# Two SSM layers of a two-block network: the powers of B and the zeroing of the lag table moved from VectorE to GpSimd, with new task tables

## What is computed

```python
h = rmsnorm(x, norm_mix[i])
proj = h @ w_in[i]
q, k, v, cb, cc, cx, u, g = jnp.split(proj, IN_SPLITS, axis=-1)
q, k = partial_rope(q, ...), partial_rope(k, ...)
y_attn = sliding_window_attention(q, k, v, attn_sinks[i]) @ w_attn_o[i]
y_conv = (cb * short_conv(cc * cx, conv_w[i])) @ w_conv_o[i]
ys = jax.nn.gelu(s5_ssm(u, ssm_a_re[i], ssm_a_im[i], ssm_b_re[i], ...))
y_ssm = (ys * jax.nn.sigmoid(ys @ w_ssm_glu[i])) @ w_ssm_o[i]
x = x + (gates[0] * y_attn + gates[1] * y_conv + gates[2] * y_ssm) @ w_mix_o[i]
h = rmsnorm(x, norm_ffn[i])
x = x + (jax.nn.silu(gt) * up) @ w_ffn_out[i]        # gt, up = split(h @ w_ffn_in[i])
```

## Time and profile before

| what | value |
|---|---|
| median of 3 runs | 2157.72 us (2156.05 to 2157.94) |
| the profiled execution | 2156.08 us |
| its span, first to last instruction | 2154.3 us |
| granted TensorE clock | 0.999 |
| PE busy | 2131.7 us, 99% |
| DVE busy | 1640.0 us, 76% |
| ACT busy | 1212.4 us, 56% |
| POOL busy | 56.4 us, 3% |

### The profile page before, as it was taken

The page is one execution under the profiler, slowest core; times in us unless marked ns, Lnnn a source line. Parts: engine busy times, 40 slices in busy tenths (PEclk is TensorE's granted clock), DMA queues, the critical chain, the costliest instruction groups (busy, mean ns, idle before and its releaser), DMA issues.

```text
span 2154.3 us, 47945 instructions
## 1 busy us (share of the span) xinstructions
PE 2131.7 (99%) x18740; PEld 2074.0 (96%) x18740; DVE 1640.0 (76%) x2626; ACT 1212.4 (56%) x1823; POOL 56.4 (3%) x54
## 2 busy tenths in 40 slices
PE   9999999999999999999999999999999999999998
PEld 8999999999999999899999999999899999999998
DVE  8997877987778766778947877766678947877764
ACT  6656544556656445446658845445446658845443
POOL 0000000000000000000002200000000002200000
PEclk9999999999999999999999999999999999999999
DMA  7444655644456556554544466556554544465553
GB/s 250 157 136 150 201 190 185 198 156 148 138 167 216 186 194 208 169 167 147 176 158 148 148 202 208 185 188 211 174 166 148 173 160 147 148 199 189 185 189 127
DMA packets 102976, 376.54 MB, mean 175 GB/s; under 512 B 11680, under 2 KB 11808, under 8 KB 102304
## 3 DMA queue, kind: packets, MB, share of 16 engines
q1 hardware_dynamic: 101664, 368.66, 52.7%
q10 hardware_dynamic: 1152, 5.58, 0.7%
HBM read 373.14 MB, written 1.05 MB: 174 GB/s over the span
## 4 chain that ended last, share of the span: by engine, by line
PE 90%; DVE 6%; ACT 2%; issue 1%; DMA 0%; DVEq 0%; ACTq 0%
PE acc L772 25%; PE acc L774 24%; PE acc L773 24%; DVE w_lo L1806 2%; PE acc L891 1%; PE acc L893 1%; PE acc L892 1%; PE acc L836 1%; PE acc L838 1%; PE acc L837 1%; ACT w_hi L1325 1%; PE mid L1128 1%; PE mid L1227 1%; DVE pr L2565 0%; PE mid L959 0%
## 5 line engine op out<-in xcount | busy, mean ns | idle before, releaser
L1806 DVE TENSOR_TENSOR w_lo<-w_raw,w_hi 128x1024 fp32r<-128x1024 f32 x694 | 847.8, 1226 | 321.5 <-ACT w_hi L1325 313.3
L1325 ACT CAST w_hi<-w_raw 128x1024 fp32r<-128x1024 f32 x694 | 723.8, 1046 | 541.2 <-PE acc L774 476.6
L772 PE MATMUL acc<-h_hi,w_hi 128*128 128x256 f32 x2096 | 600.1, 286 | 0.1
L773 PE MATMUL acc<-h_lo,w_hi 128*128 128x256 f32 x2096 | 589.3, 281 | 0.0
L774 PE MATMUL acc<-h_hi,w_lo 128*128 128x256 f32 x2096 | 586.2, 280 | 0.0
L772 PE MATMUL acc<-g_hi,w_hi 128*128 128x256 f32 x1456 | 412.6, 283 | 0.8 <-DVE w_lo L1806 0.7
L773 PE MATMUL acc<-g_lo,w_hi 128*128 128x256 f32 x1456 | 407.9, 280 | 0.0
L774 PE MATMUL acc<-g_hi,w_lo 128*128 128x256 f32 x1456 | 407.6, 280 | 0.0
L772 PEld LDWEIGHTS acc<-h_hi,w_hi 128*128 128x128 f32 x2096 | 394.0, 188 | 6.3 <-issue 5.0
L774 PEld LDWEIGHTS acc<-h_hi,w_lo 128*128 128x128 f32 x2096 | 396.1, 189 | 0.0
L773 PEld LDWEIGHTS acc<-h_lo,w_hi 128*128 128x128 f32 x2096 | 395.5, 189 | 0.5
(11 more groups left out here) (443 smaller groups left out, 3454.6 us busy)
## 6 DMA issues: line engine op xcount, KB each, us to landing
w_raw<-weights_d SPq DMA_DIRECT2D x695, 512.0 KB, 3.6
p<-p_d ACTq DMA_DIRECT2D x3, 1080.0 KB, 8.5
rdec<-decay_d ACTq DMA_DIRECT2D x2, 768.0 KB, 7.6
p<-p_d SPq DMA_DIRECT2D x1, 1024.0 KB, 10.8
out_d<-work SPq DMA_DIRECT2D x4, 256.0 KB, 2.3
x_all<-x_d SPq DMA_DIRECT2D x1, 516.0 KB, 4.4
w_raw<-weights_d SPq DMA_DIRECT2D x2, 256.0 KB, 5.8
x_all<-x_d SPq DMA_DIRECT2D x1, 512.0 KB, 6.2
```

The source lines that it names most:

```text
L772: mm(dst, wh, hi[:, k, :], start=first and j == 0, stop=False)
L773: mm(dst, wh, lo[:, k, :], start=False, stop=False)
L1325: nc.scalar.copy(w_hi[:, slot, :], w_raw[:, slot, :]).then_inc(hi_done, 1)
L1806: tt(w_lo[:, slot, :], w_raw[:, slot, :], w_hi[:, slot, :].bitcast(F32), SUB).then_inc(lo_v, 1)
```

## The change

The powers 1 to 3 of B are made by GpSimd, by the same four operations each, in a list of its own ahead of its work for the second block. It waits for a new semaphore `v_fac`, which DVE's reciprocal at L2056 (the line after the last factor) raises, for B and C to have landed, and for the last raw slab. TensorE's `tr` 0 waits for the new `p_power`. The lag table is now a tile of 16x3x32 columns on the parameters of B and C, which are read by then: GpSimd zeroes it as soon as the powers, power 0 on ACT and the table from C on DVE are done, and `lag_copy` waits for `p_lag` and for the matmuls. DVE has neither `power` nor `lag_zero` any more. Both tables of tasks are new, with the same tasks otherwise.

```diff
-        lag = in_arena("lag", 91136, [P, PAIRS, STEP, PC])
+        lag = place("lag", [P, PAIRS, STEP - 1, PC], at=p_at + 4 * P1["b_re"][0])
...
+            mine = Products()
+            times = nc.gpsimd.tensor_tensor
+            def power(at, p):
+                i = STEP - 1 - p
...
+                times(by_re, b, l_re, ALU.mult)
+                times(by_im, b, l_im, ALU.mult).then_inc(p_step, 1)
+                pool.wait_ge(p_step, mine.next())
+                times(bs[0][:, :, i, :], by_re[:, 0, :, :], by_im[:, 1, :, :], ALU.subtract)
+                times(bs[1][:, :, i, :], by_re[:, 1, :, :], by_im[:, 0, :, :], ALU.add).then_inc(p_power, 1)
+                pool.wait_ge(p_power, at.n * 3 + p)
+            def powers(at):
+                if at.n == 0:
+                    pool.wait_ge(params, 16)
+                pool.wait_ge(v_fac, at.n + 1)
+                wait_used(pool, at, raw_end(at.n) - 1)
+                for p in range(1, STEP):
+                    power(at, p)
+            def lag_zero(at):
+                pool.wait_ge(a_power, at.n * 2 + 2)
+                pool.wait_ge(v_prep, at.n * 3 + 3)
+                nc.gpsimd.memset(lag[:, :, :, :], 0.0).then_inc(p_lag, 1)
+            for n in range(DEPTH):
+                at = Layer(False, n)
+                powers(at)
+                lag_zero(at)
...
-                    pe.wait_ge(v_power, at.n * 3 + 3)
+                    pe.wait_ge(p_power, at.n * 3 + 3)
...
-                act.wait_ge(v_lag, at.n + 1)
+                if j == 0:
+                    act.wait_ge(p_lag, at.n + 1)
+                    act.wait_ge(pe_lag, at.n + 1)
...
-                nc.vector.reciprocal(tiny[:, 17, :], tiny[:, 16, :])
+                nc.vector.reciprocal(tiny[:, 17, :], tiny[:, 16, :]).then_inc(v_fac, 1)
```

Of the tables, the entries up to the recurrence, layer 0:

```diff
-        3: (("mean",), ("roots",), ("h", 0), ("h", 1), ("h", 2), ("h", 3), ("lows",)),
-        5: (("rope", 0),),
-        6: (("rope", 1),),
-        7: (("prep_d",), ("rope", 2)),
-        9: (("scaled",),),
-        10: (("rope_mul", 0),),
+        3: (("mean",),),
+        4: (("roots",),),
+        6: (("h", 0), ("h", 1), ("h", 2), ("h", 3), ("lows",)),
+        9: (("prep_d",),),
         12: (("out_table",),),
-        14: (("power", 0),),
-        15: (("rope", 3), ("rope_mul", 1)),
-        17: (("rope", 4),),
-        18: (("double", 0), ("double", 1)),
-        19: (("rope_mul", 2),),
-        21: (("vt",), ("vt_copy",), ("power", 1)),
-        22: (("rope_mul", 3), ("rope_mul", 4)),
-        23: (("spread", 0),),
-        24: (("power", 2),),
-        26: (("power", 3), ("spread", 1), ("spread", 2), ("spread", 3)),
-        27: (("double", 2),),
-        28: (("tr", 0), ("tr", 1), ("tr", 2), ("tr", 3), ("tr", 4), ("double", 3), ("double", 4), ("tr", 5),
-            ("tr", 6), ("tr", 7), ("tr_copy", 0), ("tr_copy", 1), ("tr_copy", 2), ("tr_copy", 3), ("tr_copy", 4),
-            ("tr_copy", 5), ("tr_copy", 6), ("lag",), ("bu", 0), ("tr_copy", 7), ("lag_zero",), ("lag_copy", 0),
-            ("lag_copy", 1), ("double", 5), ("lag_copy", 2)),
-        29: (("bu", 1), ("rot", 0), ("bu", 2), ("bu", 3), ("rot", 1)),
-        30: (("rot", 2), ("rot", 3)),
...
+        3: (("mean",),),
+        4: (("roots",),),
+        6: (("h", 0), ("h", 1), ("h", 2), ("h", 3), ("lows",)),
+        9: (("prep_d",),),
         12: (("out_table",),),
-        14: (("power", 0),),
-        15: (("rope", 3), ("rope_mul", 1)),
-        17: (("rope", 4),),
-        18: (("double", 0), ("double", 1)),
-        19: (("rope_mul", 2),),
-        21: (("vt",), ("vt_copy",), ("power", 1)),
-        22: (("rope_mul", 3), ("rope_mul", 4)),
-        23: (("spread", 0),),
-        24: (("power", 2),),
-        26: (("power", 3), ("spread", 1), ("spread", 2), ("spread", 3)),
-        27: (("double", 2),),
-        28: (("tr", 0), ("tr", 1), ("tr", 2), ("tr", 3), ("tr", 4), ("double", 3), ("double", 4), ("tr", 5),
-            ("tr", 6), ("tr", 7), ("tr_copy", 0), ("tr_copy", 1), ("tr_copy", 2), ("tr_copy", 3), ("tr_copy", 4),
-            ("tr_copy", 5), ("tr_copy", 6), ("lag",), ("bu", 0), ("tr_copy", 7), ("lag_zero",), ("lag_copy", 0),
-            ("lag_copy", 1), ("double", 5), ("lag_copy", 2)),
-        29: (("bu", 1), ("rot", 0), ("bu", 2), ("bu", 3), ("rot", 1)),
-        30: (("rot", 2), ("rot", 3)),
-        31: (("scores", 0), ("mask", 0), ("scan",)),
-        33: (("scores", 1), ("scores", 2)),
-        34: (("mask", 1),),
-        35: (("mask", 2), ("scores", 3), ("mask", 3), ("scores", 4)),
-        36: (("mask", 4), ("turn",), ("scores", 5)),
-        38: (("scores", 6), ("scores", 7), ("mask", 5)),
-        39: (("mask", 6), ("mask", 7)),
-        40: (("out_power", 1), ("maxima",)),
+        13: (("power", 0),),
+        14: (("scaled",), ("rope", 0), ("rope", 1)),
+        15: (("rope", 2),),
+        16: (("rope_mul", 0),),
+        18: (("rope_mul", 1),),
+        19: (("rope", 3),),
+        21: (("rope", 4), ("rope_mul", 2), ("vt",), ("vt_copy",)),
+        22: (("rope_mul", 3), ("double", 0)),
+        23: (("rope_mul", 4), ("double", 1)),
+        24: (("tr", 0), ("double", 2), ("double", 3), ("tr_copy", 0)),
+        25: (("double", 4),),
+        26: (("tr", 1), ("tr", 2), ("tr_copy", 1), ("tr_copy", 2), ("spread", 0), ("tr", 3), ("tr_copy", 3)),
+        27: (("double", 5), ("tr", 4), ("tr", 5), ("tr_copy", 4), ("tr", 6), ("tr_copy", 5), ("tr_copy", 6),
+            ("spread", 1), ("spread", 2), ("spread", 3), ("tr", 7), ("tr_copy", 7)),
+        28: (("lag_copy", 0), ("lag_copy", 1), ("lag",), ("lag_copy", 2)),
+        29: (("bu", 0), ("bu", 1), ("bu", 2), ("bu", 3)),
+        30: (("rot", 0), ("rot", 1), ("rot", 2), ("rot", 3)),
...
```

Layer 1:

```diff
-        1: (("mean",), ("roots",)),
-        3: (("scaled",), ("h", 0), ("h", 1), ("h", 2), ("h", 3), ("lows",)),
-        4: (("rope", 0), ("rope_mul", 0), ("rope", 1)),
-        5: (("power", 0), ("rope_mul", 1)),
-        7: (("rope", 2), ("rope", 3)),
-        8: (("rope_mul", 2), ("power", 1)),
-        9: (("rope_mul", 3), ("spread", 0), ("rope", 4)),
-        10: (("rope_mul", 4), ("vt",), ("vt_copy",)),
-        11: (("spread", 1), ("power", 2)),
-        13: (("power", 3),),
-        16: (("tr", 0), ("tr", 1), ("tr", 2), ("tr_copy", 0)),
-        17: (("tr_copy", 1),),
-        18: (("tr_copy", 2), ("tr", 3), ("tr_copy", 3), ("tr", 4), ("tr_copy", 4), ("tr", 5), ("tr_copy", 5)),
-        20: (("tr", 6), ("tr", 7), ("lag",), ("spread", 2), ("spread", 3), ("tr_copy", 6), ("tr_copy", 7),
-            ("lag_zero",)),
-        21: (("bu", 0), ("bu", 1), ("rot", 0), ("lag_copy", 0), ("lag_copy", 1), ("lag_copy", 2)),
...
+        1: (("mean",), ("roots",), ("power", 0)),
+        2: (("rope", 0),),
+        3: (("h", 0), ("h", 1), ("h", 2), ("h", 3), ("lows",)),
+        4: (("scaled",), ("rope", 1), ("rope", 2)),
+        5: (("rope_mul", 0),),
+        6: (("rope_mul", 1),),
+        8: (("rope", 3),),
+        9: (("spread", 0),),
+        10: (("rope_mul", 2), ("rope", 4), ("vt",), ("spread", 1), ("vt_copy",)),
+        12: (("rope_mul", 3), ("rope_mul", 4)),
+        14: (("tr", 0),),
+        16: (("tr", 1), ("tr", 2), ("spread", 2), ("tr_copy", 0)),
+        17: (("tr_copy", 1), ("tr_copy", 2), ("tr", 3)),
+        19: (("tr_copy", 3), ("tr", 4), ("tr_copy", 4), ("tr", 5), ("tr_copy", 5), ("tr", 6), ("tr_copy", 6)),
+        20: (("spread", 3), ("tr", 7)),
+        21: (("tr_copy", 7), ("lag",), ("bu", 0), ("rot", 0), ("lag_copy", 0), ("lag_copy", 1), ("bu", 1),
+            ("rot", 1), ("lag_copy", 2)),
+        22: (("bu", 2), ("rot", 2), ("bu", 3)),
...
```

More of the change, by code:

```diff
@@ L160 @@
-        41: (("out_power", 2),),
[L161 to L167, removed]
@@ new lines @@
+        41: (("out_power", 2),),
+        42: (("softmax",), ("out_power", 3), ("normalize",)),
+        45: (("cx",), ("ssm_y",)),
+        46: (("gelu",), ("gelu_lo",)),
+        47: (("pt", 0), ("pt", 1), ("pt_copy", 0), ("pt_copy", 1)),
+        48: (("pv", 0), ("pv", 1)),
+        49: (("pt", 2), ("pt_copy", 2), ("pv_lo", 0), ("pt", 3), ("pv_copy", 0), ("pt_copy", 3)),
+        50: (("pv", 2), ("pv", 3), ("pv_copy", 1), ("pv_lo", 1), ("pt", 4), ("pt", 5), ("pt_copy", 4),
+            ("pt_copy", 5), ("pv_lo", 2), ("pv_lo", 3)),
@@ new lines @@
+        51: (("pv", 4), ("pv", 5), ("pv_copy", 2), ("pt", 6), ("pt_copy", 6), ("pt", 7), ("pt_copy", 7), ("pv", 6),
+            ("pv", 7), ("pv_copy", 3)),
+    },
+    {
+        1: (("mean",), ("roots",), ("power", 0)),
[16 more added lines that the diff above has]
+        22: (("bu", 2), ("rot", 2), ("bu", 3)),
+        24: (("rot", 3),),
+        26: (("scan",),),
+        29: (("scores", 0), ("mask", 0)),
+        30: (("turn",), ("scores", 1), ("scores", 2)),
+        32: (("mask", 1), ("mask", 2), ("scores", 3), ("mask", 3)),
+        34: (("scores", 4), ("mask", 4), ("scores", 5), ("scores", 6), ("mask", 5), ("mask", 6)),
+        36: (("scores", 7), ("mask", 7)),
+        37: (("out_power", 1), ("maxima",)),
```

(57 more changed lines are left out.)

27 lines of the change are left out of this document (8 added, 19 removed), and 4 rows, old and new, of the table ORDER1.

## The result

The changed kernel takes 2178.06 us (median of 4 runs, 2177.28 to 2179.2) beside 2157.83 for the kernel before: +20.2 us, a ratio of 1.0098 with a 95% interval of 1.0084 to 1.0111. The forecast was 2182, +25.8 on the profiled execution. The profiled execution of after took 2178.27 us (+22.2 on that of before), its span 2176.2 at a granted clock of 0.996.

What follows compares the result with a forecast made beforehand. PE's slab pace was taken to bound the kernel, with DVE nearly keeping it waiting. 27.1 us lateness - 1.2 - 0.7 + 0.6 = +25.8 on 2156.1 gave 2182 us; 8-in-10 range 2153 to 2198.

Steps and rivals of the forecast that it cites:

- What bounds: First layers: PE's slab pace, 2.8 us per slab, is the floor; DVE nearly keeps it waiting; 1.9 us to win.
- Powers and memset leave DVE: Each layer: DVE is freed of 12.8 us, worth at most 0.7 us of w_lo waits to the end.
- The same work on GpSimd: Each layer: a 1024-column product takes 2.65 us, a 512-column sum 1.29, the three powers 23.6 us on GpSimd.
- The share that DVE loses: Beside GpSimd, DVE loses 0.85 of a product and 1.09 us of each sum, 19.8 us per layer.
- Layer 0: Slab 16 comes 17.2 us late, 19.8 lost less a 2.6 us lead; 15.2 after taking off 2.
- the 2 us taken off for PSUM readers: Each layer: 2 us less lateness, for DVE operations reading PSUM, about one in seven, that run beside GpSimd.
- Layer 1: Around slab 10: 13.9 us late, 19.8 lost less a 5.9 us lead; 11.9 after taking off 2.
- Tables: New task order: the 1.2 us wait at tr goes, extra breaks in the slab stream cost 0.6, bu in a row nothing.
- 2: GpSimd dearer, 4 us per 1024 columns: DVE loses 27 us per layer, +40, 2196 us; chance 0.12.
- 3: No slower: DVE's turns cost less than its lead ahead of slabs 16 and 10; 2152 to 2155 us; chance 0.16.
- 4: The change misses the path: GpSimd starts late enough to meet DVE with full lead; 2156 us; chance 0.10 with the rest.
- Rival 1: Engines meet only part of the time: DVE loses 55%, 13 us per layer, +16, 2172 us; chance 0.17.

Runs made afterwards that it cites:

- no_powers: The kernel after with its new tables, but GpSimd zeroes powers 1 to 3 with two memsets instead of multiplying: 2155.57 us (before 2156.2), ratio 0.9998.
- engine_alone: The task tables of the kernel before, with GpSimd making the powers and the memset as in after: 2184.89 us (before 2157.18), ratio 1.0126.
- memsets: The kernel after with each GpSimd product and sum replaced by a memset, which reads nothing: 2155.25 us (before 2156.2), ratio 0.9995.

## Why the prediction was right, point by point

*What bounds.* Right: the pace of slabs is the floor, and the lead of DVE is what is lost. The list of what the first layers lose was too short: the same view has PE waiting there for 1.4 us at L941, 1.3 at L979, 0.5 at L976 (issue) and 1.1 for `probt` at L1035. None of it entered the sum.

*Powers and memset leave DVE.* Worth at most 0.7 us, I said; `no_powers` gains 0.6 in all, no more than noise. The memset took 1.38 us on GpSimd, between the bounds, and disturbed nobody.

*The same work on GpSimd.* This term was mis-sized: a 1024-column product takes 1.92 to 1.99 us undisturbed, not 2.65. I extended a line through 256 and 512 columns whose two points were different operations, a product and a sum. The estimate from the Trainium skill ("GPSIMD Engine Reference", Performance versus the Vector engine), 2.2 us, was nearer. The sums took 1.26 to 1.36, as taken. Twelve operations make 6 x 1.95 + 6 x 1.31 = 19.6 us instead of 23.6. So the sign "31 or more as recorded" failed: GpSimd was busy 24.5 us in layer 0 and 27.6 in layer 1, the memset included.

*The share that DVE loses.* Nearly right. `w_lo` of slab 16 is ready at 54.35 us in `no_powers` and at 69.67 in after, 15.3 us later; the stretches of the DVE operations ahead of it sum to 15.2. That is 78% of 19.6; I had taken 85%. The whole-instruction rule of the Trainium skill ("SBUF — State Buffer", Who interferes with whom), by which all 19.6 would be lost, is right in kind (a 16-column operation waits for a whole product) and 4.3 us high in the sum.

*Layer 0.* Forecast 15.2 before the 1.3 for the tables. By the same steps with the measured product: 6 x 1.95 x 0.85 + 6 x 1.09 = 16.5; DVE lost 15.3. The lead in `no_powers` is 2.24, so slab 16 is 15.3 - 2.2 = 13.1 us late there. To this come 1.8 us for the clock, which no step of mine had: 14.9 behind `no_powers` at slab 17, and 14.5 at the end of the layer. So the dear product made this term 3.3 us too high, the missing clock 1.8 too low, and the share, the lead and the 2 us taken off for PSUM readers together 1.2 too low. That they nearly cancel is luck. Taking something off for PSUM readers was right in kind (L2304).

*Layer 1.* Forecast 11.9, measured 7.4. `w_lo` of slab 10 is ready at 481.28 us, 28.07 behind `no_powers`, 14.5 of it from layer 0, so DVE lost 13.5 there, not 19.8. Its lead in `no_powers` is 5.5, which leaves 8.0, beside holes of 7.8 by starts (1.53, 1.27, 1.61, 3.40). The dear product made the term 3.3 us too high. A miscount made it 2.2 too high: I had put all twelve of GpSimd's operations ahead of that `w_lo`, and the trace has ten. The 2 us taken off for PSUM readers went the other way. The last two operations stand beside `w_lo` of slabs 10 to 13:
```profile
478.36 8.51 DVE L1857 TENSOR_TENSOR w_lo<-w_raw,w_hi 128x1024 fp32r<-128x1024 f32 x4
```
```profile
480.28 2.14 POOL L739 TENSOR_TENSOR bs_re<-tm 128x512 f32<-128x512 f32 x1
482.38 2.26 POOL L740 TENSOR_TENSOR bs_im<-tm 128x512 f32<-128x512 f32 x1
```
They stretch `w_lo` of slabs 11 and 12 to 2.3 us each, which PE doesn't wait for. Ten operations make 6 x 1.95 + 4 x 1.31 = 16.9 us, and 13.5 is 80% of that, the share of layer 0. GpSimd also lost its first turn:
```profile
458.08 3.73 POOL L736 TENSOR_TENSOR tm<-p,fac 128x1024 f32<-128x1024 f32 x1 [388.02 <-PE acc L823]
```
Beside it four `h_lo` of DVE ran undisturbed (2.49 us together), so the expected lateness inside slab 5 didn't come. It did with the old table (`engine_alone`, 4.4 us on `h_lo`).

*Tables.* The wait of 1.2 us at `tr` is gone. But I had taken 1.3 us off in all, and `no_powers` ends layer 0 only 0.1 us ahead of before and the whole 0.6: something took the gain back, and its wait for `w_lo`, 1.1 us where before has 0.7, is only a part of it. That the tables were needed in layer 1, where they save 8.5 us beside the products, I hadn't seen: I had costed them apart from the engine.

*Rivals.* 2 is out with the product at 1.95 us, 3 with the 1.78 of L2113, 4 with GpSimd's starts at 43 and 458 us, where DVE's lead doesn't cover the loss. Rival 1's 13 us per layer comes near the 13.5 of layer 1, but not for its reason: DVE had no idle time there while GpSimd worked, it was busy 26.8 of the 27 us from 458 to 485.

## What to carry to other kernels

Moving work to GpSimd unloaded DVE here only where DVE beside it read PSUM (0.41 us stayed 0.41) or where GpSimd only wrote (`memsets`). Against a product even an operation on a single tile was held up (L2307, 1.55 us instead of 0.35). So 12.8 us of DVE work became 15.3 us of lost DVE time, ahead of the tightest slab. Ask first what is won if the work vanishes altogether: a run that leaves it out answered 0.6 us, not told from nothing. And when a table and an engine change together, neither half alone has a meaningful price, because each puts the other's consumers in a new place.
